# A two-block transformer kernel on one core: the expert stage's coefficient groups, index transposes, Gelu table and two one-hot groups are placed ahead of the last TensorE row

## What is computed

```python
def peer_ffn(h, w_q, sub_keys, expert_u, expert_v):     # (bsz, seq, d) = (1, 256, 2048)
    q = (h @ w_q).reshape(bsz, seq, PEER_HEADS, 2, PEER_HALF_DIM)
    scores = jnp.einsum('bshpd,hpnd->bshpn', q, sub_keys)
    sv, si = lax.top_k(scores, PEER_TOPK)                # 8 heads, 2 halves, 16 of 128 keys
    ...
    eidx = jnp.take_along_axis(cidx, tp, axis=-1)        # 8 x 16 = 128 experts of 16384 per token
    gw = jax.nn.softmax(tv, axis=-1)
    def chunk(args):                                     # 128 tokens at a time
        xc, ic, wc = args
        a = jnp.einsum('td,ted->te', xc, expert_u[ic])
        a = jax.nn.gelu(a, approximate=False) * wc
        return jnp.einsum('te,ted->td', a, expert_v[ic])
```

## Time and profile before

| what | value |
|---|---|
| median of 3 runs | 2939.76 us (2936.44 to 2942.71) |
| the profiled execution, its own time | 2940.28 us |
| its span in the trace | 2938.5 us |
| busy: TensorE matmul / weight load | 2657.4 / 2065.1 us (90 / 70%) |
| busy: VectorE / ScalarE / GpSimd | 2160.4 / 607.9 / 902.9 us (74 / 21 / 31%) |
| DMA | 935.12 MB, mean 318 GB/s |

### The profile page before, as it was taken

One profiled execution on the slowest core, in us unless ns is written; L12 is line 12 of the kernel. 1 busy time (PEld: TensorE's weight loads), 2 busy tenths in 40 slices (PEclk: granted clock), 3 DMA queues, 4 the chain that ended last, 5 costly groups with the idle time before them and its releaser, 6 DMA issues.

```text
span 2938.5 us, 31053 instructions
## 1 busy us (share of the span) xinstructions
PE 2657.4 (90%) x11792; PEld 2065.1 (70%) x11792; DVE 2160.4 (74%) x2978; ACT 607.9 (21%) x1279; POOL 902.9 (31%) x712
## 2 busy tenths in 40 slices
PE   6999999999999999999999998767666768999997
PEld 5888778755686688578657687766666655666664
DVE  6797576687896657425677869999999878656667
ACT  1121240200100210122000121212377776000000
POOL 1100001000000100000000025777777657666665
PEclk8999999999999999999999999888877779999998
DMA  9954479788787644424878679999999988999998
GB/s 403 421 207 144 171 261 412 300 306 352 274 335 306 258 143 144 143 101 190 355 272 325 244 304 416 421 421 421 419 419 420 402 326 292 403 413 414 413 414 346
DMA packets 147736, 935.12 MB, mean 318 GB/s; under 512 B 16400, under 2 KB 16656, under 8 KB 53136
## 3 DMA queue, kind: packets, MB, share of 16 engines
q0 software_dynamic: 101376, 604.02, 51.4%
q1 hardware_dynamic: 44784, 320.66, 28.3%
q10 hardware_dynamic: 1440, 8.59, 0.7%
HBM read 929.02 MB, written 4.19 MB: 318 GB/s over the span
## 4 chain that ended last, share of the span: by engine, by line
PE 52%; DMA 22%; DVE 10%; ACT 7%; POOL 5%; issue 3%; DVEq 0%; SPq 0%
PE G L584 28%; PE M L908 7%; DMA acc<-v_rows,proj 6%; DMA aring<-ada 4%; DMA mix<-v_rows,proj 4%; PE B L908 3%; DMA vec<-peer_u,proj 3%; ACT vec L1598 2%; DMA proj<-v_rows,proj 2%; PE M L1176 2%; DMA aring<-peer_u,proj 2%; DVE vec L2534 2%; POOL aring L556 2%; PE G L908 2%; DVE aring L2506 2%
## 5 line engine op out<-in xcount | busy, mean ns | idle before, releaser
L584 PE MATMUL G<-h,ring 128*128 128x256 f32 x3264 | 716.6, 380 | 0.5 <-ACT h L1312 0.2
L584 PEld LDWEIGHTS G<-h,ring 128*128 128x128 f32 x3264 | 616.8, 190 | 92.8 <-issue 7.9
L541 POOL DMA_DIRECT2D aring<-ada x176 | 93.1, 529 | 1475.5 <-DVE mods L1729 1427.0
L1729 DVE CUSTOM_DVE_ANT_0 aring<-aring,acc,vec 128x2048 f32<-128x2048 f32 x160 | 372.3, 2350 | 57.9 <-DMA aring<-ada 54.9
L584 PE MATMUL G<-proj,ring 128*128 128x256 f32 x1472 | 322.7, 381 | 2.6 <-DVE proj L2075 1.7
L584 PEld LDWEIGHTS G<-proj,ring 128*128 128x128 f32 x1472 | 279.8, 191 | 43.6 <-issue 3.4
L1223 PE MATMUL M<-sq,mix 128*128 128x512 f32 x688 | 301.4, 594 | 0.0
L556 POOL DMA_INDIRECT aring<-peer_u,proj x130 | 233.6, 1797 | 199.0 <-DVE dots L2506 81.7
L1223 PEld LDWEIGHTS M<-sq,mix 128*128 128x128 f32 x688 | 203.6, 297 | 89.3 <-ACT mix L1612 0.7
L2534 DVE SCALAR_TENSOR_TENSOR vec<-acc,dots,vec 128x1024 f32<-128x1024 f32 x149 | 191.4, 1284 | 97.4 <-DMA acc<-v_rows,proj 92.2
L2506 DVE CUSTOM_DVE_ANT_0 aring<-sq,aring 128x2048 f32<-128x2048 f32 x104 | 236.4, 2291 | 32.1 <-DMA aring<-peer_u,proj 21.3
(11 more groups left out here) (496 smaller groups left out, 3658.5 us busy)
## 6 DMA issues: line engine op xcount, KB each, us to landing
ring<-weights SPq DMA_DIRECT2D x219, 1024.0 KB, 5.5
aring<-ada POOLq DMA_DIRECT2D x176, 1024.0 KB, 9.1
sq<-v_blocks SPq DMA_DIRECT2D x43, 1024.0 KB, 8.0
proj<-v_blocks SPq DMA_DIRECT2D x21, 1024.0 KB, 8.0
ring<-first SPq DMA_DIRECT2D x16, 896.0 KB, 11.1
sq<-ada POOLq DMA_DIRECT2D x8, 1024.0 KB, 20.2
acc<-ada POOLq DMA_DIRECT2D x4, 1024.0 KB, 18.5
proj<-ada POOLq DMA_DIRECT2D x4, 1024.0 KB, 22.2
```

Of the source, the lines that this page charges most:

```text
L541: pool.dma_start(ada_at(n), ada[n]).then_inc(ada_in[ada_slot(n)], 16)
L584: mm = nc.tensor.matmul(bank[:, 0:TOK], lhsT=ring[:, slot, weights_at + t * P:weights_at + (t + 1) * P], rhs=rhs[:, t, :], start=(t == ord ...
L1729: V_.tensor_tensor_reduce(out=tile, in0=tile, in1=vector, scale=1.0, scalar=bias, op0=ALU.mult, op1=ALU.add, accum_out=column).then_inc(ad ...
```

## The change

Six things are done; nothing is computed that was not computed before, but for one Gelu of a constant that is not used.

- `spreads_after` spreads block 0's 32 groups over 20 rows, 144 to 239. Row 244 has none.
- ScalarE does the last `keep_mix` of block 0 and `keep_picks(1)` behind row 239's groups; TensorE does `turn_picks(1)` ahead of row 244.
- Behind `gate_exp(1)` ScalarE runs a Gelu on one column, with the table load that this needs.
- VectorE marks the groups 0 and 1 of block 1 behind the dots of the rows 248 and 252, each after a wait for `turned_kept` to reach 3, which is when `keep_picks(1)` has ended. It marked both behind `coefficients(1)` before.
- Row 244's diagonal is read behind row 255's dot, no longer behind row 252's.
- VectorE's wait for `turned_kept` to reach 4 ahead of the burst is gone.

```diff
 READ_BEHIND = {n: n + (6 if n in TURN_EARLY else 8) for n in [*TURN_EARLY, *TURN_LATE]}
+READ_BEHIND[TURN_LATE[-1]] = 2 * NSLOT - 1
 EXP_AT = 222
+MARKED_AT = {248: 0, 252: 1}
...
         def spreads_after(n):
-            late = pe_rows_before(2 * NSLOT) - pe_rows_before(NSLOT + SEL)
+            late = len(TURN_LATE) - 1
             i = pe_rows_before(n) - pe_rows_before(NSLOT + SEL)
+            if i == late:
+                return range(0)
             return range(P // 4 * i // late, P // 4 * (i + 1) // late)
...
             for n in range(NSLOT + SEL, 2 * NSLOT):
+                if n == TURN_LATE[-1]:
+                    turn_picks(1)
                 if on_pe(n):
                     turn_and_dot(n)
                     for g in spreads_after(n):
                         spread_coefs(0, g)
-            turn_picks(1)
             turn_coefs(1)
...
                         one_hots(g)
                         if g > 0:
                             keep_mix(0, g - 1)
+                    if n == TURN_LATE[-2]:
+                        keep_mix(0, P // 4 - 1)
+                        keep_picks(1)
                 if n == EXP_AT:
                     gate_exp(1)
-            keep_mix(0, P // 4 - 1)
-            keep_picks(1)
+                    nc.scalar.activation(small[:, 10:11], eps, ACT.Gelu)
             dots_gelu(1)
             keep_coefs(1)
...
                 if n == NSLOT + SEL - 1:
                     coefficients(0)
+                if n in MARKED_AT:
+                    dve.wait_ge(turned_kept, 3)
+                    one_hots(MARKED_AT[n])
             coefficients(1)
-            dve.wait_ge(turned_kept, 4)
             dve.wait_ge(mix_in, P // 4)
             in_burst = [n for n in range(P // 4 + len(V_ON_PE)) if n not in V_ON_PE]
             for g in range(P // 4):
-                one_hots(g)
+                if g >= len(MARKED_AT):
+                    one_hots(g)
                 v_add(in_burst[g])
```

## The result

The changed kernel takes 2948.34 us, median of 20 runs (2941.78 to 2952.55); the kernel before, timed beside it, 2939.61 us (20 runs, 2928.11 to 2944.98). The ratio is 1.0026, 95% interval 1.0018 to 1.0034: slower by 0.26%, or 5 to 10 us. The forecast was 2951.0 us in a range of 2945.5 to 2955.0.

What follows compares the result with a forecast made beforehand. Bound: ScalarE and TensorE handing each other work by groups, not DMA. Items 1 to 6 put `weigh_hot(0)` at 2418.0 instead of 2406.77, +11.2 us on 2940.28, so 2951.5; given as 2951.0 us for the median, range 2945.5 to 2955.0.

Steps and rivals of the forecast that it cites:

- The chain of rows and groups: From 2112.11 to 2383.76 us: TensorE and ScalarE hand each other work; a row takes 10.74 us with one group, 16.17 to 16.67 with two.
- The rival of the absorbed groups: Gathers set the pace, idle time takes the two groups, `weigh_hot(0)` comes 6.4 us earlier: 2933.4 us; chance 10%.
- Item 1: Two groups moved ahead of rows 239 and 244: row 239's transposes at 2379.0 instead of 2383.76, ends 2378.5 and 2379.4.
- Item 2: Table load behind row 219: 0.6 us stick out of ScalarE's wait and delay row 239's transposes to 2379.6.
- Item 3: Row 239's groups, last `keep_mix` and picks: 18.8 us to kept picks at 2398.4; row 244's transposes at 2398.0, 14.2 later.
- Item 4: VectorE, done with row 248's dot at 2389.5, stands until the picks are kept at 2398.4: a new wait of 9 us.
- Item 5: VectorE's two markings, seven dots and diagonal behind the kept picks: 18.1 us, ending at 2416.5 where it was 2398.1.
- Item 6: From the dots to the burst: no load or marking left, 0.05 + 1.5 us, so `weigh_hot(0)` at 2418.0.
- The sentence above the items: Start of `weigh_hot(0)`, 2406.77 us before the change, taken as the point behind which everything follows unchanged.
- Item 7: Inside the burst: counted zero, 0.6 us gain to 2 us loss; wrong if time and `weigh_hot(0)` shifts differ by over 2.
- The collision with the first blocks: Burst's start: gathers queue behind expert_v's first blocks, requested only some 1.5 us ahead instead of 8.7; up to 2 us lost.
- 7.4 without the hold: Rival: VectorE not held, row 255's late gather sets the end, `weigh_hot(0)` at 2414.2, +7.4 us, 2946.7 us; chance 10%.

Runs made afterwards that it cites:

- experiment 9: Changed kernel, but from row 144 on TensorE transposes each row ahead of the previous row's groups: 2928.62 us, ratio 0.9957 to the kernel before.
- experiment 10: Kernel before, with TensorE transposing each row ahead of the previous row's groups and nothing of the change: 2933.46 us, ratio 0.9968.
- experiment 2: Kernel before plus only the one-column Gelu, and so its table load, behind the exponential of block 1's gates: 2940.31 us, ratio 0.9996.
- experiment 1: Changed kernel, but VectorE marks groups 0 and 1 of block 1 behind coefficients(1) again, not among the dots: 2945.56 us, ratio 1.0024.
- experiment 3: Changed kernel with block 1's picks turned and kept ahead of row 234: 2945.08 us, ratio 1.0022 to the kernel before.
- experiment 4: Kernel before, groups left over 21 rows, but picks, table load, marks and Gelu early, diagonal late, coefficients in the other bank: 2936.26 us, ratio 0.9994.
- experiment 5: Kernel of experiment 4 with the first two blocks of expert_v requested later: 2939.30 us, ratio 0.9996 to the kernel before.
- experiment 11: Kernel before with only the 32 groups moved to rows 144 to 239, none behind row 244: 2945.59 us, ratio 1.0008.
- experiment 6: Changed kernel with the first two blocks of expert_v requested later: 2951.32 us, ratio 1.0034 to the kernel before.

## Why the prediction was right, and where it was off

Right by its main mechanism: the moved groups make row 244 and its slot late, and VectorE stands some 9 us for the kept picks. The total of the profiled executions, +7.9 for +11.2, is nearer than its parts, since errors of both signs meet in it. Point by point:

1. **The chain of rows and groups** is what the stretch runs on, though DMA was at 1.00 there. Experiments 9 and 10 show it: taking the handing over apart, with every operation kept, brings row 239 18 us nearer to row 144 than in the first profile of before and 7.7 nearer than in the second (236.9 for 255.0 and 244.6). One sentence of the working goes too far, that the two engines "hardly ever both run": both are recorded as busy for 117.8 of the 271.65 us. Of row 239, for one, TensorE's product and ScalarE's first one-hots lie beside each other:

```profile
2370.44 3.80 PE L1186 MATMUL B<-sq,acc 128*128 128x128 f32 x32
2371.60 2.44 ACT L1598 ACTIVATE vec<-cst 128x128 f32<-128x128 f32 x8
```

What is in series is ScalarE's own work (two halves copied, 2.7 us with the 0.68 between them, and 5.3 a group) and its wait for the next transposes (2.45 or 3.39): some 16.7 us for a row with two groups. The rival of the absorbed groups is out; where the gathers do set the pace, in experiments 9 and 10, the groups are absorbed, as it said.

2. **Item 1, row 239 at 2379.0 (2379.6 with the load): came at 2375.00.** This is the term that was mis-sized. 19 rows with 30 groups took 259.2 us, where the working's paces give 267.5 with the load. At the lower clock level the forecast nearly holds (the changed kernel without marks: 265.4), at the higher one a row is 1.2 to 1.6 us shorter, and in this execution some rows were. Against it, row 144 itself came 3.67 us later, ahead of anything that the change touches; that the miss is 4.6 us and not 8.3 is luck. The prediction's own sign for a wrong item 1, a start before 2375, was just missed at 2375.00, and is clearly there if one counts from row 144 (262.9 us at that sign, 259.2 measured). The working took the pace of one execution as the kernel's own; the second profile of before (244.6 for 255.0) shows that this sum has a spread of 10 us that the ends of item 1 (0.9 us apart) did not have.

3. **Item 2, the table load:** 0.6 us sticking out. The first copy for row 224 started 0.59 us later than its wait of 2.45 would have let it (2333.51 + 2.45 = 2335.96, and it came at 2336.55); the one-column Gelu took 0.20. The agreement is partly luck: 2.45 us is the wait at the lower clock level, and row 224's transposes took 1.91 us here, the higher level. TensorE then waited 1.72 us for the copy, and the row took 16.45 us to the next where rows with two groups at that level took 15.06: the two loads cost some 1.4 us in this execution, an estimate from these two. Where two groups stand ahead of it, at the lower clock level, the load costs nothing (experiment 2). No load here is followed by a gap: 0.01 to 0.04 us to the next instruction. By the Trainium skill, "ScalarE: Activation LUTs", section What ACT_TABLE_LOAD costs, each switch costs a drain of about 1.38 us on top of the load; the traces have none, behind a load or ahead of it (2333.51 to 2333.52, 2335.13 to 2335.15).

4. **Item 3,** row 239's transposes to kept picks 18.8 us: 18.80. **Item 4,** the wait of 9 us: 8.87. **Item 5,** 18.1 us from the kept picks to the diagonal: 18.09. **Item 6,** from there to `weigh_hot(0)` 1.55: 1.61. The hold came 4.6 us earlier as a whole, as item 1 did.

5. **The sentence above the items failed: that `weigh_hot(0)` is the point from which the rest follows unchanged.** The burst took 77.35 us in the first profile of before, 81.2 in the second, 79.6 and 81.4 in the two of after, and 77.35 to 83.62 over all 13 profiles. No other single instant ahead of the burst does better: the burst ends 77.4 to 83.6 us behind `weigh_hot(0)`, 81.4 to 88.9 behind the last dot (81.4 and 83.2 in the changed kernel, 85 to 86 in both profiles of before), and 93.0 to 100.3 behind the issue of row 255's gather. Two things go with its length. Where `weigh_hot(0)` came less than 14 us behind the issue of row 255's gather (experiments 1, 3, 4, 5 and 11) the burst took 81.1 to 83.6 us, in the other eight profiles, at 16 to 19 us, 77.4 to 81.4. And TensorE's granted clock in it was highest in the shortest burst (0.95) and lowest in the longest (0.84, experiment 4). No run separates the two, nor tells whether the lower clock lengthens the burst or comes of it; and the two profiles of before, both at 19.11 us, show that the gather's lead isn't all. While VectorE is held, GpSimd's first gathers of expert_v go on (2398.38 to 2410.27, all issued before the last dot was done at 2411.67); that this pays back a part of the hold is my reading. The steadier point is the burst's end, for which TensorE's further products wait: from there to the end of the span it took 454.4 us before, 453.3 after, 450.6 to 455.8 over all 13.

   **Item 7** is undecided by its own sign: the span moved by 1.2 us more than `weigh_hot(0)` did (7.9 for 6.7), under its 2 us; the burst alone took 2.2 more, just over its upper bound. The collision with the first blocks, its reason, is not the cause (experiments 5 and 6).

6. **What the parts cost.** The moved groups cost some 2 to 7 us (experiment 11 at 1.0008; experiments 1 and 3, which have the groups moved and no hold but other parts of the change too, at 1.0024 and 1.0022). The hold costs what is left of 1.0026, 0 to 3 us, which the times can't tell from zero. The forecast had 7.4 without the hold and 11.2 with it (2946.7 stands beside the 7.4; by its own terms that is 2947.2). The order of the two was right, both were some 2 to 3 us too high: item 1 was too high by 4.6, and the burst gave part of it back.

7. **The changed order's hoped-for gain** was to take picks, load and marking out of the steps behind the last dot. It did: from the diagonal to `weigh_hot(0)` there is 1.6 us. But in the kernel before these steps waited for groups that were late anyhow (`weigh_hot(0)` 8.7 us behind the last dot in one profile, 3.9 in the other), and putting the groups ahead of row 244 moved the slot, the last gather and the last dot instead.

## What to carry to other kernels

A stretch in which DMA is at 1.00 and two engines at 70% can still run at the pace of those two, if each waits for the other: compare the time from one round to the next between rounds with more and with less of the work, before you call their idle time room. Work that is put ahead of an instruction which frees a buffer costs at the buffer's next user, so follow the slot and not the engine; here the cheap way was to let the freeing instruction (the transposes) pass the work in question. And a point from which "the rest follows unchanged" has to be tried on two executions of the same kernel: if it moves and the end doesn't, it is not that point. Two profiles also give the size below which an instant read from one of them proves nothing, 5.8 to 10.6 us here.

## What was not expected of the hardware

Two executions of one program differed by 10.6 us in a stretch of 270 us (271.7 and 261.1), with the same operations, through stretches of TensorE at 2.4 GHz in one and at 1.2 GHz in the other, and the whole differed by 0.5 us. Ahead of the transposes shown at 1.00 (row 169) TensorE had done row 164's transposes, its product with the tokens and one group; ahead of those at 0.50 (row 174) row 169's transposes, product and two groups, with waits of 1.83 and 3.97 us ahead of the groups; the level fell in the first group, from 1.00 up to 2188.5 us to 0.50 from 2189 on. But row 169's transposes, with the same work ahead of them, took 1.91 us in this execution and 3.05 in the other, so the order of the work doesn't settle the level.

VectorE's dots ran at a pitch of 2.21 us when nothing held them and at 2.48 us behind gathers of 1 MB each; so by an estimate from the two seven held dots catch up 1.9 us (7 x 0.27) of a hold by themselves.
